# Feed forward: 24 of 32 inner tiles as twelve pairs of seven products each, kept in memory and loaded by output chunk

## The chip, the cores and the metric

One core of one Trainium2 chip. The metric is the device time of one execution, in microseconds (us). TensorE is called PE below, VectorE DVE, ScalarE ACT, GpSimd POOL and SyncE SP; SP issues most of the DMAs.

## What is computed

Two transformer-like blocks on one sequence of 1024 tokens by 1024 channels, all in fp32. The part that is changed is the feed forward of the first block, in the reference:

```
h = rmsnorm(x, norm_mlp_pre[l])
f = jnp.square(jax.nn.relu(h @ w_ff_in[l])) @ w_ff_out[l]
x = x + rmsnorm(f, norm_mlp_post[l])
```

`w_ff_in` is 1024 by 4096 and `w_ff_out` 4096 by 1024. The second block, behind it, has a wide projection of its own (`h @ w_in`), of which the kernel already forms a part with seven products instead of eight.

## The kernel before, in words

**Numbers.** Each fp32 operand is split in a high part (a rounded copy, made by ACT) and a low part (what is left, one subtraction on DVE). A product is three matmuls: high by high, high by low, low by high. Every matmul has a 128x128 stationary operand and 512 moving columns.

**Inner tiles.** An inner tile `("fi", T)` holds 128 of the 4096 inner channels for all 1024 tokens. The stationary operand is a slice of `w_ff_in`, the moving one the tokens `XBH`, `XBL` (high and low, in two halves of 512 tokens). `tile` (L2031) issues 8 depth slices x 2 halves x 3 = 48 matmuls (L2005 to L2007). It is then evicted on a chain of four steps, each of which waits for the one before: ACT relu from PSUM to `HS` (L1112), DVE square (L1628), ACT high copy to `H` (L1114), DVE low part (L1631). `H` has five places of one tile.

**Output chunks.** Chunk c (of eight, `FCH`) multiplies the inner tiles 4c to 4c+3 with the matching rows of `w_ff_out`: for both halves n of the 1024 output channels and for eight token groups m, `out_part` (L2318) issues 4 x 3 = 12 matmuls into one of four PSUM banks (`BANKS4`), so 192 to a chunk. The first chunk's results are copied to `F` by ACT (L1119), the others added to `F` by DVE (`f_add`, L1614). The weights of a half n live in `W2H[n]`, `W2L[n]`; their high copy (`hi`, L842) waits until the last part of that half of the chunk before is `filled`, their low part (`lo`, L1346) follows on DVE.

**Order.** The order of each engine is written out by hand. All four engines run the same loop over c (SP L653, ACT L1094, DVE L1619, PE L2346): the tiles 4c+1 to 4c+4, then chunk c. The tile 4c+4 stands between tile 4c+3 and chunk c. In the last round the tiles 29 to 31 stand between chunk 6 and chunk 7. Chunk 7 is issued in another order: for m = 0, 1 and both n the slices 0 to 2, then the four slices 3, then m = 2 to 7. While it runs, DVE and ACT finish the block (norm, sum, norm, `f_scale`, `x2_norm`) and PE turns the tokens (`t2_turn`, L2059).

**Waits.** `filled(key)` waits until PE has finished a result, `freed(key)` until it has been evicted. The two weight slots `raw` are filled by SP (`panel`, L472), each when the low part of the panel before last is made.

**The seven products.** In the second block `seven(p)` (L2427) makes two tiles of 128 channels from seven products of 512 tokens by 512 depth, 12 matmuls each (L2441 to L2443), 84 in place of 96. This needs four sums of token quarters, made once (`token_sum`, `TR` raw, `TH` high, `TL` low, each 128x2048), and four sums of weight quarters for each pair (`seven_sums`, `S`, 128x512). ACT copies three of the products to `c1`, `c5`, `c2`, DVE adds those to later ones into `stage` (three buffers of one tile), ACT applies the function, and SP stores the tile (`gate_store`). The weights of seven products go through a ring of four places (`seven_hi`, `seven_lo`).

## Time and profile before

| | us |
|---|---|
| median of 3 runs | 2179.26 (2177.72 to 2179.93) |
| the profiled execution's own time | 2176.35 |
| its span in the trace | 2174.6 |
| PE busy | 2140.1 |
| DVE busy | 1047.2 |
| ACT busy | 696.0 |
| mean DMA rate | 99 GB/s |

The feed forward runs from about 635 us (first inner tile) to about 1326 us (last output part), the seven products of the second block from 1471 to 1852 us. PE's busy time is of pipelined matmuls: a matmul is recorded with 0.39 us, though the next one starts 0.23 us after it. How fast PE works is read from the starts. The granted clock is 0.998 of full speed over the span.

### The profile page before, as it was taken

To read this page: it belongs to the slowest core of one execution; us is meant where nothing else is said; L and a number is where in the kernel's file an instruction comes from. 1 tells how busy PE (TensorE), PEld (TensorE's weight loads), DVE (VectorE), ACT (ScalarE), POOL (GpSimd) and SP (SyncE) were. 2 spreads that over 40 slices of the span, in tenths; PEclk is the share of its full clock that TensorE was granted. 3 is DMA by queue.
4 is the path that set the end of the run, shared out by engine and by line. 5 is a ranking of instruction groups with operands and counts; after the bars stand their busy time and mean duration, and the time that the engine had idled before them with its cause. 6 is when DMAs were issued, how large, how long until landed. Compare 5 with 4: busy or idle time off the path is not lost.

```text
span 2174.6 us, 24357 instructions
## 1 busy us (share of the span) xinstructions
PE 2140.1 (98%) x9972; PEld 1771.0 (81%) x9972; DVE 1047.2 (48%) x1170; ACT 696.0 (32%) x988; POOL 266.0 (12%) x507
## 2 busy tenths in 40 slices
PE   7999999999999999999999999999999999999998
PEld 6888888877888888888888888888888888878877
DVE  4226666847442233233232357666444566535452
ACT  4246666153233212112021135214444332222121
POOL 1376295000100000000000012100000000000100
PEclk9999999999999999999999999999999999999999
DMA  6542333676312012011020143212333221424332
GB/s 160 110 107 95 113 99 119 162 246 232 119 49 78 20 58 78 20 59 58 20 77 20 58 174 114 67 39 106 108 116 112 82 78 45 164 80 163 116 117 106
DMA packets 161922, 214.50 MB, mean 99 GB/s; under 512 B 26099, under 2 KB 127124, under 8 KB 161556
## 3 DMA queue, kind: packets, MB, share of 16 engines
q1 hardware_dynamic: 152336, 190.28, 26.9%
q10 hardware_dynamic: 9476, 22.67, 3.2%
q8 instruction: 79, 1.29, 0.2%
q14 instruction: 31, 0.25, 0.0%
HBM read 164.03 MB, written 47.71 MB: 97 GB/s over the span
## 4 chain that ended last, share of the span: by engine, by line
PE 86%; DVE 5%; issue 4%; ACT 2%; DMA 1%; SPq 1%; POOL 1%; DVEq 0%; POOLq 0%; ACTq 0%
PE A L2005 11%; PE A L2006 11%; PE A L2007 11%; PE X L2267 6%; PE X L2269 6%; PE X L2268 6%; PE X L2441 3%; PE X L2443 3%; PE X L2442 3%; PE A L2443 3%; PE A L2442 3%; PE A L2441 3%; PE A L2267 2%; PE A L2269 2%; PE A L2268 2%
## 5 line engine op out<-in xcount | busy, mean ns | idle before, releaser
L1339 DVE TENSOR_TENSOR WL<-raw,WH 128x1024 fp32r<-128x1024 f32 (+1 forms) x134 | 144.4, 1078 | 294.5 <-ACT WH L836 294.4
L2005 PE MATMUL A<-XBH,WH 128*128 128x512 f32 x616 | 240.1, 390 | 0.5 <-DVE WL L1339 0.5
L2007 PE MATMUL A<-XBH,WL 128*128 128x512 f32 x616 | 239.7, 389 | 0.0
L2006 PE MATMUL A<-XBL,WH 128*128 128x512 f32 x616 | 239.7, 389 | 0.0
L836 ACT ACTIVATE WH<-raw 128x1024 fp32r<-128x1024 f32 (+1 forms) x134 | 122.3, 913 | 282.4 <-PE A L2007 159.3
L2267 PE MATMUL X<-W2H,H 128*128 128x512 f32 x512 | 199.5, 390 | 0.0
L2269 PE MATMUL X<-W2H,H 128*128 128x512 f32 x512 | 199.2, 389 | 0.0
L2268 PE MATMUL X<-W2L,H 128*128 128x512 f32 x512 | 199.2, 389 | 0.0
L1112 ACT ACTIVATE HS<-A 128x1024 f32<-128x1024 f32 x32 | 32.8, 1024 | 400.9 <-PE A L2007 395.0
L2005 PE MATMUL A<-XH,WH 128*128 128x512 f32 x384 | 151.7, 395 | 0.0
L1618 DVE TENSOR_TENSOR F<-F,X 128x512 f32<-128x512 f32 x112 | 75.6, 685 | 156.3 <-PE X L2269 154.3
L2007 PE MATMUL A<-XH,WL 128*128 128x512 f32 x384 | 149.6, 390 | 0.0
L2006 PE MATMUL A<-XL,WH 128*128 128x512 f32 x384 | 149.5, 389 | 0.0
L2005 PEld LDWEIGHTS A<-XBH,WH 128*128 128x128 f32 x616 | 115.6, 188 | 25.0 <-issue 1.1
L2007 PEld LDWEIGHTS A<-XBH,WL 128*128 128x128 f32 x616 | 115.6, 188 | 24.1
L2006 PEld LDWEIGHTS A<-XBL,WH 128*128 128x128 f32 x616 | 115.6, 188 | 23.8
L1628 DVE TENSOR_TENSOR HS<-HS 128x1024 f32<-128x1024 f32 x32 | 39.1, 1223 | 171.7 <-ACT HS L1112 171.7
L2269 PEld LDWEIGHTS X<-W2H,H 128*128 128x128 f32 x512 | 96.1, 188 | 20.0
L2268 PEld LDWEIGHTS X<-W2L,H 128*128 128x128 f32 x512 | 96.1, 188 | 19.9
L2267 PEld LDWEIGHTS X<-W2H,H 128*128 128x128 f32 x512 | 96.1, 188 | 19.8
L1353 DVE TENSOR_TENSOR WL<-S,WH 128x512 fp32r<-128x512 f32 x80 | 55.1, 689 | 71.9 <-ACT WH L860 71.1
L2694 POOL TENSOR_TENSOR M<-M,GB 128x1024 f32<-128x1024 f32 x4 | 9.6, 2394 | 632.4 <-DVE GB L1919 632.4
(532 smaller groups left out, 4621.9 us busy)
## 6 DMA issues: line engine op xcount, KB each, us to landing
raw<-in_w_in SPq DMA_DIRECT2D x49, 1024.0 KB, 5.2
raw<-in_w_ff_in SPq DMA_DIRECT2D x16, 1024.0 KB, 5.4
rawk<-in_w_ff_out SPq DMA_DIRECT2D x16, 1024.0 KB, 5.0
g_scr<-stage SPq DMA_DIRECT2D x24, 512.0 KB, 3.6
g_scr<-gst ACTq DMA_DIRECT2D x32, 256.0 KB, 2.8
x_scr<-xr ACTq DMA_DIRECT2D x16, 512.0 KB, 2.6
xr<-x_scr SPq DMA_DIRECT2D x16, 512.0 KB, 4.2
xtok<-in_x SPq DMA_DIRECT2D x8, 512.0 KB, 7.4
```

What stands on the lines that cost most here:

```text
L836: A(unit_home(WH[:, r % 2, 0:kb, :], key), unit_of(raw[:, SLOT[p], 0:kb, :], key, i), ACT.Copy).then_inc(w_hi, 1)
L1339: TT(unit_home(WL[:, r, 0:kb, :], key), unit_of(raw[:, SLOT[p], 0:kb, :], key, i), unit_home(WH[:, r, 0:kb, :], key).bitcast(f32), ALU.sub ...
L1618: TT(F[:, m, sl], F[:, m, sl], psum(("fo", c, n, m)), ALU.add).then_inc(evicted[BUF["fo", c, n, m]], 1)
L2005: mm(dst, WH[:, r, k, :], xh, start=(k == 0), stop=False)
L2006: mm(dst, WH[:, r, k, :], xl, start=False, stop=False)
L2007: return mm(dst, WL[:, r, k, :], xh, start=False, stop=(k == kb - 1))
L2267: mm(dst, xh, wh(k), start=(k == 0), stop=False)
L2268: mm(dst, xh, wl(k), start=False, stop=False)
L2269: last = mm(dst, xl, wh(k), start=False, stop=(k == kb - 1))
L2441: mm(psum(key), high[:, i, :], xh, start=opens and i == 0, stop=False, skip_group_check=not opens)
L2442: mm(psum(key), high[:, i, :], xl, start=False, stop=False, skip_group_check=not opens)
L2443: last = mm(psum(key), low[:, i, :], xh, start=False, stop=i == KW - 1, skip_group_check=not opens)
```

## The change

Inner tiles 4 to 27 are made by `seven(p)`, p = 0 to 11, two to a pair; the tiles 0 to 3 (first) and 28 to 31 (last) stay plain. All 32 inner tiles are made before the first output chunk. The tiles 0 to 27 are evicted to `stage`, with relu on ACT and the square on DVE in place, and stored by SP to `h_scr` in memory, 512 KB each. Chunk 0 now uses the tiles 28 to 31, which stay in the SBUF; chunk c = 1 to 7 uses the tiles 4(c-1) to 4(c-1)+3, which SP loads (`h_load`) to `HBS`, where the tokens were, or to `HS`. ACT and DVE make their high and low parts in the middle of the chunk before, behind the weights of its first half. The token sums are formed on DVE during the plain tiles 0 to 3, each quarter from its high and low part (`rejoined`). In the second block the numbering of pairs and stages is shifted, its order is not. What is left out below is the counterpart of `seven_act`, `seven_dve` and `seven_func` for the new kind "f", and this shift.

```diff
-for _c in range(FCH):
-    if _c == 0:
-        pair("fi", 4)
-    if _c + 1 < FCH:
-        PANELS.append(([("fi", 4 * _c + 4), ("fi", 4 * _c + 5)], 1))
-    PANELS.append(([("w2", 2 * _c)], 1))
-    PANELS.append(([("w2", 2 * _c + 1)], 1))
-    if _c + 1 < FCH:
-        PANELS.append(([("fi", 4 * _c + 6), ("fi", 4 * _c + 7)], 1))
...
+SEVEN = [("f", i, 0) for i in range(2, 14)]
+SEVEN += [("g", s, i) for s in range(3) for i in range(4)] + [("b", i, kind) for i in range(2) for kind in range(4)]
+LAST_HIDDEN = 28
+
+RUNS = ((range(0, 12), "fi", (("fi", LAST_HIDDEN), ("fi", LAST_HIDDEN + 1))), (range(12, 32), "az", (("cx", 0), ("cx", 1))))
...
+pair("fi", 4)
+seven_panels(RUNS[0])
+for _i in range(LAST_HIDDEN, 4 * FCH, 2):
+    PANELS.append(([("fi", _i), ("fi", _i + 1)], 1))
+single("w2", 2 * FCH)
...
+FILLS += seven_fills(RUNS[0], (("A0a", "A0b", "X1a"), ("X0a", "X0b", "X1b")))
+FILLS += [(("fi", t), "A%d" % (t % 2)) for t in range(LAST_HIDDEN, 4 * FCH)]
...
-    FILLS += [(("fi", t), "A%d" % (t % 2)) for t in range(4 * _c + 5, min(4 * _c + 9, 4 * FCH))]
...
+        h_scr = dram("h_scr", [FF, SEQ])
...
+        def hidden_of(raw_form, u):
+
+            c, i = u // 4, u % 4
+            if c in (0, 2, 4, 7):
+                return (HS if raw_form else H)[:, (3, 4, 1, 0)[i]]
+            return (HBS if raw_form else HB)[:, i + (4 if c == 6 else 0)]
...
             def w2_panel(c, n):
-                panel(("w2", 2 * c + n), wf2[:, KW * c:KW * (c + 1), W4 * n:W4 * (n + 1)])
+                g = (c - 1) % FCH
+                panel(("w2", 2 * c + n), wf2[:, KW * g:KW * (g + 1), W4 * n:W4 * (n + 1)])
...
+            def h_store(T):
+                sp.wait_ge(hs_ready, T + 1)
+                sp.dma_start(h_scr[T * P:(T + 1) * P, :], stage[T % 3][:]).then_inc(x1_out[T % 3], 16)
+
+            def h_load(c):
+                if c in (2, 3, 4, 5, 7):
+                    filled(sp, ("fo", c - 3 if c == 7 else c - 2, 1, MT - 1))
+                for u in range(4 * c, 4 * c + 4):
+                    T = u - 4
+                    staged(sp, T % 3, T // 3 + 1)
+                    sp.dma_start(hidden_of(True, u)[:, 1, :], h_scr[T * P:(T + 1) * P, :]).then_inc(h_in[c % 2], 16)
+            for p in RUNS[0][0]:
+                seven_panel(p, wf1, 2 * P * (p + 2))
+                h_store(2 * p)
+                h_store(2 * p + 1)
+            fi_panel(LAST_HIDDEN)
+            h_store(LAST_HIDDEN - 4)
+            h_store(LAST_HIDDEN - 3)
+            fi_panel(LAST_HIDDEN + 2)
+            w2_panel(0, 0)
+            h_store(LAST_HIDDEN - 2)
+            h_store(LAST_HIDDEN - 1)
+            w2_panel(0, 1)
+            filled(sp, ("fi", 4 * FCH - 1))
+            for c in range(1, FCH):
+                h_load(c)
                 w2_panel(c, 0)
                 w2_panel(c, 1)
-                if c + 1 < FCH:
-                    fi_panel(4 * c + 6)
...
+            def hidden_stage(T):
+                filled(act, ("fi", T))
+                if T == 0:
+                    freed(act, ("t1", 7))
+                    for i in range(3):
+                        act.wait_ge(x1_out[i], STORED1[i])
+                staged(act, T % 3, T // 3)
+                A(stage[T % 3][:], psum(("fi", T)), ACT.Relu).then_inc(evicted[BUF["fi", T]], 1)
+            hi(("fi", 2))
+            hidden_stage(0)
+            sum_high(0, 0)
+            hi(("fi", 3))
+            hidden_stage(1)
+            sum_high(0, 1)
+            sum_high(0, 2)
+            seven_hi(0, 0)
+            seven_hi(0, 1)
+            hidden_stage(2)
+            sum_high(0, 3)
+            seven_hi(0, 2)
+            seven_hi(0, 3)
+            hidden_stage(3)
+            seven_run(0, None)
+
+            def hidden_high(u):
+                home = hidden_of(True, u)[:, 1, :]
+                if u < 4:
+                    act.wait_ge(hs_ready, LAST_HIDDEN + u + 1)
+                else:
+                    hidden_in(act, u // 4)
+                A(hidden_of(False, u)[:, 0, :], home, ACT.Copy).then_inc(hidden_hi, 1)
+            for i in range(3):
+                staged(act, i, (10, 9, 9)[i])
+            for u in range(4):
+                key = ("fi", LAST_HIDDEN + u)
+                if u in (1, 2):
+                    hi(("fi", LAST_HIDDEN + u + 1))
+                if u >= 2:
+                    hi(("w2", u - 2))
+                filled(act, key)
+                A(hidden_of(True, u)[:, 1, :], psum(key), ACT.Relu).then_inc(evicted[BUF[key]], 1)
+                hidden_high(u)
+            for c in range(FCH - 1):
+                for n in range(2):
+                    if c == 0:
                         for m in range(MT):
-                            filled(act, ("fo", 0, n, m))
-                            A(F[:, m, W4 * n:W4 * (n + 1)], psum(("fo", 0, n, m)), ACT.Copy
-                              ).then_inc(evicted[BUF["fo", 0, n, m]], 1)
+                            key = ("fo", 0, n, m)
+                            filled(act, key)
+                            A(F[:, m, W4 * n:W4 * (n + 1)], psum(key), ACT.Copy).then_inc(evicted[BUF[key]], 1)
+                    filled(act, ("fo", c, n, MT - 1))
+                    hi(("w2", 2 * (c + 1) + n))
+                    if n == 0:
+                        for u in range(4 * c + 4, 4 * c + 8):
+                            hidden_high(u)
             hi(("au", 0))
...
+            def hidden_square(T):
+                if T < 4:
+                    freed(dve, ("fi", T))
+                else:
+                    p, h = (T - 4) // 2, T % 2
+                    dve.wait_ge(stage_done, 3 * p + 3)
+                    if h:
+                        freed(dve, ("P", p, 6))
+                S = stage[T % 3][:]
+                TT(S, S, S, ALU.mult).then_inc(hs_ready, 1)
...
-            for c in range(FCH):
-                for T in range(0 if c == 0 else 4 * c + 1, min(4 * c + 5, 4 * FCH)):
-                    if T:
-                        follow(("fi", T))
-                    if T == min(4 * c + 4, 4 * FCH - 1):
-                        for n in range(2):
-                            lo(("w2", 2 * c + n))
-                    freed(dve, ("fi", T))
-                    S = HS[:, T % 5, 1, :]
-                    TT(S, S, S, ALU.mult).then_inc(hs_ready, 1)
-                    dve.wait_ge(hidden_hi, T + 1)
-                    dve.wait_ge(hs_ready, T + 1)
-                    TT(H[:, T % 5, 1, :], S, H[:, T % 5, 0, :].bitcast(f32), ALU.subtract).then_inc(hidden_lo, 1)
-                if 0 < c < FCH - 1:
-                    for n in range(2):
...
+            def quarter(t, k, h):
+                return t[:, h, KW * k:KW * k + KW, :].bitcast(f32)
+
+            def rejoined(dst, k, h):
+                return mark(TT(dst[:], quarter(XBH, k, h), quarter(XBL, k, h), ALU.add))
+
+            def sum_low(n, count):
+                dve.wait_ge(t_high, count)
+                TT(TL[n][:], TR[n][:], TH[n][:].bitcast(f32), ALU.subtract).then_inc(t_low, 1)
+            for m in (6, 7):
+                freed(dve, ("t1", m))
+            rejoined(TD[0], 0, 1)
+            link(TT(TD[1][:], quarter(XBH, 0, 0), quarter(XBL, 0, 0), ALU.add))
+            mark(TT(TR[0][:], TD[0][:], TD[1][:], ALU.subtract))
+            lo(("fi", 2))
+            hidden_square(0)
+            link(TT(TD[2][:], quarter(XBH, 1, 1), quarter(XBL, 1, 1), ALU.add))
+            TT(TR[2][:], TD[2][:], TD[0][:], ALU.subtract).then_inc(t_raw, 1)
+            dve.wait_ge(t_raw, 1)
+            TT(TR[1][:], TR[2][:], TD[1][:], ALU.add).then_inc(t_raw, 1)
+            lo(("fi", 3))
+            sum_low(0, 1)
+            hidden_square(1)
+            rejoined(TD[3], 1, 0)
+            after(chain[0])
+            dve.wait_ge(t_raw, 2)
+            TT(TR[3][:], TD[3][:], TR[1][:], ALU.subtract).then_inc(t_raw, 1)
+            dve.wait_ge(t_raw, 3)
+            sum_low(1, 2)
+            seven_sums(0, (0, 1))
+            seven_lo(0, 0)
+            seven_lo(0, 1)
+            sum_low(2, 3)
+            hidden_square(2)
+            seven_sums(0, (2, 3))
+            sum_low(3, 4)
+            seven_lo(0, 2)
+            seven_lo(0, 3)
+            hidden_square(3)
+            seven_run(0)
...
+            for u in range(4):
+                key = ("fi", LAST_HIDDEN + u)
+                if u in (1, 2):
+                    lo(("fi", LAST_HIDDEN + u + 1))
+                if u >= 2:
+                    lo(("w2", u - 2))
+                if u == 0:
+                    for T in (LAST_HIDDEN - 2, LAST_HIDDEN - 1):
+                        hidden_square(T)
+                freed(dve, key)
+                S = hidden_of(True, u)[:, 1, :]
+                TT(S, S, S, ALU.mult).then_inc(hs_ready, 1)
+                hidden_low(u)
+            for c in range(FCH - 1):
+                for n in range(2):
+                    if c:
                         for m in range(MT):
                             f_add(c, n, m)
+                    lo(("w2", 2 * (c + 1) + n))
+                    if n == 0:
+                        for u in range(4 * c + 4, 4 * c + 8):
+                            hidden_low(u)
             lo(("au", 0))
             lo(("au", 1))
 
...
                     pe.wait_ge(w_lo, UNIT["w2", 2 * c + n] + 1)
 
                 def tokens(k, m):
-                    s = (4 * c + k) % 5
-                    return H[:, s, 0, P * m:P * (m + 1)], H[:, s, 1, P * m:P * (m + 1)]
+                    home = hidden_of(False, 4 * c + k)
+                    return home[:, 0, P * m:P * (m + 1)], home[:, 1, P * m:P * (m + 1)]
 
                 def hidden(k):
...
-            for c in range(FCH):
-                for T in range(2 if c == 0 else 4 * c + 1, min(4 * c + 5, 4 * FCH)):
-                    tile(("fi", T), xb)
-                if c < FCH - 1:
-                    for n in range(2):
-                        for m in range(MT):
-                            out_part(c, n, m)
+            tile(("fi", 2), xb)
+            tile(("fi", 3), xb)
+            for p in RUNS[0][0]:
+                seven(p)
+            for T in range(LAST_HIDDEN, 4 * FCH):
+                if T == LAST_HIDDEN:
+                    for b in ("A0a", "A0b"):
+                        free_of(b, ("fi", T))
+                tile(("fi", T), xb)
+            for c in range(FCH - 1):
+                for n in range(2):
+                    for m in range(MT):
+                        out_part(c, n, m)
```

**DVE where the inner tiles begin.** `TD`, `TR`, `TL` are the token sums, `S` the weight sums, `WL` low parts of weights, `stage` an inner tile. Before, behind the last `XBL`:

```order
L1386 TENSOR_TENSOR XBL<-X,XBH 128x8x128 [waits xt_hi] x2
L1628 TENSOR_TENSOR HS<-HS 128x1024 [waits evicted_A0]
L1631 TENSOR_TENSOR H<-HS,H 128x1024 [waits hidden_squared,hidden_hi]
L1339 TENSOR_TENSOR WL<-raw,WH 128x1024 [waits w_hi]
L1628 TENSOR_TENSOR HS<-HS 128x1024 [waits evicted_A1]
L1631 TENSOR_TENSOR H<-HS,H 128x1024 [waits hidden_squared,hidden_hi]
L1339 TENSOR_TENSOR WL<-raw,WH 128x1024 [waits w_hi]
```

and with the change:

```order
L1816 TENSOR_TENSOR TD_198<-XBH,XBL 128x2048 [waits evicted_X1,evicted_X0]
L1824 TENSOR_TENSOR TD_199<-XBH,XBL 128x2048
L1825 TENSOR_TENSOR TR_190<-TD_198,TD_199 128x2048 [waits dve_chain]
L1427 TENSOR_TENSOR WL<-raw,WH 128x1024 [waits w_hi]
L1769 TENSOR_TENSOR stage_209<-stage_209 128x1024 [waits evicted_A0]
L1828 TENSOR_TENSOR TD_200<-XBH,XBL 128x2048
L1829 TENSOR_TENSOR TR_192<-TD_200,TD_198 128x2048 [waits dve_chain]
L1831 TENSOR_TENSOR TR_191<-TR_192,TD_199 128x2048 [waits t_sum]
L1427 TENSOR_TENSOR WL<-raw,WH 128x1024 [waits w_hi]
L1820 TENSOR_TENSOR TL_194<-TR_190,TH_186 128x2048 [waits t_hi]
L1769 TENSOR_TENSOR stage_210<-stage_210 128x1024 [waits evicted_A1]
L1816 TENSOR_TENSOR TD_201<-XBH,XBL 128x2048
```

Between the last token turn and the low weights of tile 2 there are now three operations of 2048 columns, and before the low weights of the third product (`WL<-S_203,WH`) there are twelve of them.

**DVE from the last plain tile to the first output chunks, with the change.** `HS` to `H` is the chain of an inner tile that stays in the SBUF, `HBS` to `HB` that of loaded tiles.

```order
L1434 TENSOR_TENSOR W2L<-rawk,W2H 128x2048 [waits w_hi]
L1870 TENSOR_TENSOR HS<-HS 128x1024 [waits evicted_A1]
L1857 TENSOR_TENSOR H<-HS,H 128x1024 [waits hidden_squared,hidden_hi]
L1434 TENSOR_TENSOR W2L<-rawk,W2H 128x2048 [waits w_hi]
L1857 TENSOR_TENSOR HB<-HBS,HB 128x1024 [waits hidden_hi] x4
L1434 TENSOR_TENSOR W2L<-rawk,W2H 128x2048 [waits w_hi]
L1810 TENSOR_TENSOR F<-F,X 128x512 [waits evicted_X0a,tile_done]
L1810 TENSOR_TENSOR F<-F,X 128x512 [waits evicted_X0b,tile_done]
```

The chain of tile 31 is the last thing ahead of chunk 0; before, one more tile stood between. The four loaded tiles stand between the weights of one half and the sums `F<-F,X` of the next.

**DVE at the last output chunk.** Before:

```order
L1346 TENSOR_TENSOR W2L<-rawk,W2H 128x2048 [waits w_hi] x2
L1628 TENSOR_TENSOR HS<-HS 128x1024 [waits evicted_A1]
L1631 TENSOR_TENSOR H<-HS,H 128x1024 [waits hidden_squared,hidden_hi]
L1339 TENSOR_TENSOR WL<-raw,WH 128x1024 [waits w_hi] x2
L1618 TENSOR_TENSOR F<-F,X 128x512 [waits evicted_X0a,tile_done,rows2_loaded]
```

and with the change:

```order
L1810 TENSOR_TENSOR F<-F,X 128x512 [waits evicted_X1b,tile_done]
L1434 TENSOR_TENSOR W2L<-rawk,W2H 128x2048 [waits w_hi]
L1427 TENSOR_TENSOR WL<-raw,WH 128x1024 [waits w_hi] x2
L1810 TENSOR_TENSOR F<-F,X 128x512 [waits evicted_X0a,tile_done,rows2_loaded]
L1810 TENSOR_TENSOR F<-F,X 128x512 [waits evicted_X0a,tile_done]
```

The low weights of half 1 of chunk 7 (`W2L`) and the two of `("au", 0)`, `("au", 1)` (`WL`) stood among the last inner tiles, and now stand directly behind the last sum of chunk 6. On ACT the high copies stand likewise. On SP the loads of `post2`, `pre3` and the `au` panel wait for the end of chunk 6, as before; three inner tiles came between that and chunk 7, and now none does.

## Rows read from the trace of the kernel before

**Rows 1.** The page's part 1: engine, busy us (share of span), instructions.
```profile
PE 2140.1 (98%) x9972; PEld 1771.0 (81%) x9972; DVE 1047.2 (48%) x1170; ACT 696.0 (32%) x988; POOL 266.0 (12%) x507
```

**Rows 2.** Windows: stretch, length, busy us of each engine, PEclk, DMA share, GB/s.
```profile
640.00:1278.00 638.00, 637.48 (x2813) 527.55 (x2812) 210.41 (x204) 131.44 (x125) 0.00 (x0) 1.00 0.15 51
1471.00:1852.00 381.00, 381.00 (x1682) 315.24 (x1680) 211.97 (x310) 149.38 (x257) 0.00 (x0) 1.00 0.27 95
```

**Rows 3.** PE's waits, 640 to 1345: us in total, times, longest.
```profile
PE A L2059 <- DVE F L1647: 0.5, 1, 0.5
PE A L2005 <- DVE WL L1339: 0.5, 1, 0.5
```

**Rows 4.** Timeline of PE in an inner tile: start, length, instruction; 36 matmuls apart.
```profile
665.79 0.39 PE L2005 MATMUL A<-XBH,WH 128*128 128x512 f32 x1
...
673.95 0.39 PE L2005 MATMUL A<-XBH,WH 128*128 128x512 f32 x1
```

**Rows 5.** Timeline of DVE where the inner tiles begin; in brackets the idle time before.
```profile
634.91 1.22 DVE L1386 TENSOR_TENSOR XBL<-X,XBH 128x1024 fp32r<-128x1024 f32 x1 [3.51 <-ACT XBH L879]
...
645.28 1.22 DVE L1339 TENSOR_TENSOR WL<-raw,WH 128x1024 fp32r<-128x1024 f32 x1
```

**Rows 6.** Timeline of ACT there and at the first output chunk.
```profile
646.17 1.02 ACT L1112 ACTIVATE HS<-A 128x1024 f32<-128x1024 f32 x1 [1.11 <-PE A L2007]
...
668.71 1.03 ACT L1112 ACTIVATE HS<-A 128x1024 f32<-128x1024 f32 x1 [6.55 <-PE A L2007]
671.03 1.06 ACT L1114 ACTIVATE H<-HS 128x1024 fp32r<-128x1024 f32 x1 [1.29 <-DVE HS L1628]
...
679.62 1.92 ACT L842 ACTIVATE W2H<-rawk 128x2048 fp32r<-128x2048 f32 x1 [4.77 <-PE A L2007]
```

**Rows 7.** Timeline of DVE where the second block prepares its products.
```profile
1355.81 2.28 DVE L1689 TENSOR_TENSOR TD<-XBH 128x2048 f32<-128x2048 f32 x1
1358.01 2.28 DVE L1692 TENSOR_TENSOR TR<-XBL 128x2048 f32<-128x2048 f32 x1
...
1451.60 0.69 DVE L1367 TENSOR_TENSOR S<-raw 128x512 f32<-128x512 f32 x1
```

**Rows 8.** The page's part 6, one issue: count, KB each, median us to landing.
```profile
g_scr<-stage SPq DMA_DIRECT2D x24, 512.0 KB, 3.6
```

**Rows 9.** Timeline of DVE at the first output chunk.
```profile
669.77 1.23 DVE L1628 TENSOR_TENSOR HS<-HS 128x1024 f32<-128x1024 f32 x1 [6.17 <-ACT HS L1112]
672.12 1.22 DVE L1631 TENSOR_TENSOR H<-HS,H 128x1024 fp32r<-128x1024 f32 x1 [1.13 <-ACT H L1114]
...
681.57 2.29 DVE L1346 TENSOR_TENSOR W2L<-rawk,W2H 128x2048 fp32r<-128x2048 f32 x1 [4.40 <-ACT W2H L842]
```

**Rows 10.** Timeline of SP's queue ahead of the last output chunk.
```profile
1262.03 0.37 SPq L472 DMA_DIRECT2D rawk<-in_w_ff_out  x1
...
1262.99 0.43 SPq L662 DMA_DIRECT2D pre<-in_norm_g  x1
1274.65 0.38 SPq L472 DMA_DIRECT2D raw<-in_w_in  x1
```

**Rows 11.** DMA issues, 1262 to 1300: count, KB each, median us to landing.
```profile
pre<-in_norm_g SPq DMA_DIRECT2D x1, 512.0 KB, 6.6
```

**Rows 12.** Timeline of DVE in the last output chunk.
```profile
1286.88 1.99 DVE L1618 TENSOR_TENSOR F<-F,X 128x512 f32<-128x512 f32 x3 [1.99 <-issue]
```

**Rows 13.** Windows: GB/s (last) over one chunk's stretch, and with DMAs queued.
```profile
657.00:700.00 43.00, 43.00 (x191) 35.61 (x190) 14.11 (x10) 15.73 (x17) 0.00 (x0) 1.00 0.22 74
1264.00:1266.00 2.00, 2.00 (x10) 1.65 (x9) 0.00 (x0) 0.00 (x0) 0.00 (x0) 1.00 1.04 401
```

**Rows 14.** Window of PE after its idle time at the start: busy, PEclk, DMA.
```profile
21.00:24.00 3.00, 2.48 (x6) 0.55 1.14 184
```

**Rows 15.** Timeline of PE there: 8 matmuls, then 8 more of the same size.
```profile
21.52 3.56 PE L2013 MATMUL X<-XH,WH 128*128 128x512 f32 x8 [3.49 <-ACT XH L879]
24.92 2.01 PE L2016 MATMUL X<-XH,WL 128*128 128x512 f32 x8
```

More of the change, by code:

```diff
@@ new lines, in sum_high, with seven_act @@
+            def sum_high(run, n):
+                act.wait_ge(t_raw, (1, 2, 2, 3)[n] if run == 0 else 3 + (1, 2, 4, 4)[n])
+                A(TH[n][:], TR[n][:], ACT.Copy).then_inc(t_high, 1)
+            def seven_act(p, j):
+                kind, i, n = SEVEN[p]
+                key = ("P", p, j)
+                if j in (0, 1, 2):
+                    filled(act, key)
+                    if p != run_of(p)[0][0]:
+                        freed(act, ("P", p - 1, 3 + j))
+                    A((c1, c5, c2)[j][:], psum(key), ACT.Copy).then_inc(evicted[BUF[key]], 1)
+                if j == 6 and (kind != "b" or n in (0, 3)):
+                    filled(act, key)
+                    if kind != "b":
+                        t = stage_of(p, 1)
+                        staged(act, t % 3, t // 3)
+                        dst, func = stage[t % 3][:], ACT.Sigmoid if kind == "g" else ACT.Relu
+                    elif n == 0:
+                        act.wait_ge(b_product if i else vec_out, 2 if i else 64)
+                        dst, func = Y[:, 2 * i + 1, :], ACT.Copy
+                    else:
+                        dst, func = Y[:, 2 * (1 - i) + 1, :], ACT.Silu
+                    A(dst[:, 0:HALF], psum(key), func).then_inc(evicted[BUF[key]], 1)
@@ new lines, in seven_func @@
+            def seven_func(p, j):
+                kind, i, n = SEVEN[p]
+                if kind == "b" and n != 3:
+                    return
+                h = int(j == 4)
+                dst = stage[stage_of(p, h) % 3][:] if kind != "b" else Y[:, 2 * (1 - i) + h, :]
+                dst = dst[:, 0:HALF] if j == 3 else dst[:, HALF:SEQ]
+                freed(act, ("P", p, j))
+                A(dst, dst, {"f": ACT.Relu, "g": ACT.Sigmoid, "b": ACT.Silu}[kind]
+                  ).then_inc(b_silu if kind == "b" else stage_done, 1)
@@ new lines, in seven_run @@
+            def seven_run(r, last_sum):
+                run, name, follow_keys = RUNS[r]
+                for p in run:
+                    for j in range(7):
+                        seven_act(p, j)
+                        if last_sum and p == run[0] and j == 0:
+                            last_sum()
+                            sum_high(r, 3)
+                        q = 7 * p + j + 4
+                        if q < 7 * run.stop:
+                            seven_hi(q // 7, q % 7)
+                        elif j in (4, 6):
+                            hi(follow_keys[j // 2 - 2])
+                        if j >= 4:
+                            seven_func(p, j - 1)
@@ L1230, in _ @@
[L1230 to L1242 removed]
+                    seven_hi(12, 2 * t - 4)
@@ L2316, in _, with high_low, summed, seven @@
             end(first_half(("fi", 1), xb, "t1", 1), ("fi", 1))
+            def high_low(k, h):
+                return lambda i: (XBH[:, h, KW * k + i, :], XBL[:, h, KW * k + i, :])
+            def summed(n):
+                return lambda i: (TH[n][:, i, :], TL[n][:, i, :])
+            MOVING = (high_low(0, 0), summed(0), summed(1), high_low(1, 0), summed(2), high_low(1, 1), summed(3))
+            def seven(p):
+                run = run_of(p)[0]
+                for j in range(7):
+                    key = ("P", p, j)
+                    if p - run[0] < 2 and j < 2:
+                        b = BUF[key][:2]
+                        free_of(b, key)
+                    begin(key)
+                    if p == run[0] and j in (1, 2, 4, 6):
+                        pe.wait_ge(t_low, {1: 1, 2: 2, 4: 3, 6: 4}[j] + (4 if p else 0))
+                    pe.wait_ge(w_lo, UNIT[key] + 1)
+                    high, low = seven_home(WH, p, j), seven_home(WL, p, j)
+                    opens = j in (0, 1, 3)
+                    for i in range(KW):
+                        xh, xl = MOVING[j](i)
+                        mm(psum(key), high[:, i, :], xh, start=opens and i == 0, stop=False, skip_group_check=not opens)
+                        mm(psum(key), high[:, i, :], xl, start=False, stop=False, skip_group_check=not opens)
+                        last = mm(psum(key), low[:, i, :], xh, start=False, stop=i == KW - 1, skip_group_check=not opens)
+                    end(last, key)
             def out_part(c, n, m, ks=range(KW)):
```

385 lines of the change are left out of this document (152 added, 233 removed).

## The prediction

> **What bounds the kernel now.** I read the page's shares first: PE is busy 98% of the span, DVE 48% and ACT 32% [rows 1]. The windows say the same of both stretches that matter: in the feed forward PE is busy 637.48 of 638 us, in the seven products of the second block 381 of 381, at the full granted clock [rows 2]. Of PE's waits over the whole feed forward only one of 0.5 us lies among the inner tiles, on the low weights of tile 2; another of 0.5 us lies at the first token turn of the last chunk [rows 3]. So time here is the number of matmuls, plus whatever makes PE wait. The price of a matmul is not the recorded 0.39 us but the distance of starts: 36 matmuls lie between two starts 8.16 us apart, 0.2267 us each [rows 4]. A product of the second block costs the same (381 us for 1680 matmuls, 0.2268) [rows 2]: seven products in a row run without a gap.
>
> **The matmuls.** Twelve pairs take 84 matmuls in place of 96: 144 fewer, 144 x 0.2267 = **-32.6 us**. The output chunks keep their 1536. Everything else is what PE has to wait for.
>
> **The start (tiles 0 to 3).** PE: the relu of tile 1 starts at 646.17 [rows 6]; it starts 0.43 behind the start of a tile's last matmul (a matmul's 0.39 and 0.04), so tile 2 could start at 645.97 and waits only because its low weights run from 645.28 to 646.50 [rows 5]. With the change ACT makes the high copy before the relu of tile 0, and on DVE only three sums stand ahead: from 634.91 + 1.14, three times 2.20 gives 642.7, low weights done at 643.9. The wait goes: **-0.5**. Tile 3 then starts at 656.85, the first product at 667.73, the third at 673.17 (two products of 12 matmuls).
> DVE up to the low weights of the third product: 12 operations of 2048 columns, 5 of 1024 (two weights, three squares), 7 of 512. In the second block two of 2048 start 2.20 apart though they last 2.28; one of 512 lasts 0.69 [rows 7]. Taking 0.08 off each: 12 x 2.20 + 5 x 1.14 + 7 x 0.61 = 36.4. Seven of them read what the one ahead wrote and start about 0.1 later: 0.7. One wait on ACT: its first high sum needs the second difference (about 649.7), lasts about 1.9, as W2H does [rows 6], and the high copy of tile 3's weights stands behind it (about 652.6, where DVE is at 651.9): 0.75. From 636.05 that makes 673.9, and PE takes the product at about 674.0, not 673.17: **+0.9**. Bounds: 0, and +3, if every one of the 24 operations pays 0.1. The first product is free: its low part stands at about 666.5, and bank A0 is evicted at 666.3.
>
> **The pairs.** Each adds two squares (2 x 1.22) to DVE, whose load in the run of the second block is 212 of 381 us, or 10.6 of a pair's 19.05 [rows 2]; 13.0 fits. The squares stand behind the low weights of products 4 and 5, needed two products later. A stage buffer must have been stored before it is written again: the square of a pair's first tile is done some 6 us into the next pair, a store takes 3.6 [rows 8], the buffer is written at about 13. I cost this at nothing. If a squared tile came 3 us later DVE would stop, and with it all weights.
>
> **Tile 31 and chunk 0.** Tile 4c+4 used to cover the chain of tile 4c+3. Now chunk 0 needs tile 31 at once. The chain, as it stands for tile 3: relu 668.71, square 669.77, high copy 671.03, low part 672.12 to 673.34 [rows 6, 9], so 4.63, plus 0.43 ahead of it and 0.06 behind. PE has three slices, 9 matmuls = 2.04 us, and the distance of one more: 5.12 - 2.27 = 2.85, with 0.1 for starting again **+3.0**. Bounds 2.5 and 3.5. Behind the last pair nothing is added: the stores of tiles 26 and 27 hold ACT for about 10 us, inside tile 28's 10.9.
>
> **The middle of chunks 1 to 6.** When half 0 is filled, DVE waits for ACT's W2H, makes W2L (4.24 us from the start of W2H: 679.62, 681.57 + 2.29 [rows 6, 9]), then four low parts (4 x 1.14), then adds the first part of half 1: done about 9.9 after the last matmul's start. PE wants that bank for the fifth part, 0.23 + 4 x 2.72 = 11.1. That leaves 1.2 us: nothing, if the data are there. The loads (2.1 MB of tiles, then 1 MB of weights) have 21.8 us, 144 GB/s; with DMAs queued the trace shows 401 GB/s [rows 13].
>
> **Chunk 7.** Before, its weights were made during tiles 29 to 31. Now half 1 can only be made when chunk 6 has ended, and PE asks for it after 9 matmuls: 0.43 + 4.24 + 0.06 - 2.27 = 2.46, with 0.1 **+2.6**; bounds 2.2 and 3. On DVE the low weights of `au` follow, whose panel is requested only now, behind post2 and pre3: together 2 MB, the amount that went in 7.6 us from 1262.03 on (the last request at 1262.99 lands 6.6 later) [rows 10, 11]; before, the panel was requested at 1274.65, three microseconds ahead of chunk 7. Panel at 8.1, two high copies and low parts to 11.9. The first sum of chunk 7 was taken at 1286.88 [rows 12], 39 matmuls after the chunk's start at 1277.8; with the stop it is due at 12.0. So it just fits. As DVE sets the first token turn already (0.5 us [rows 3]), what it loses is lost: I take **+0.3**, bounds 0 and +2.
>
> **A rule on the clock.** Near the start of the trace PE idles 3.49 us; the next 8 matmuls take 3.56 us and the 8 behind them 2.01 [rows 15], at a granted clock of 0.55 over 21 to 24 us [rows 14]: part of that stretch was at 1.2 GHz, the lower level, and cost 1.5 us. The Trainium skill (TensorE: Matmul & The Clock Gate, Part 1: The HAM clock gate) says that the array falls to half clock when it has been idle and comes back once it works. By it the two new waits could each be followed by a slow stretch, and the result would be some 3 us later. In the sum I take 0, since PE was busy at full clock for hundreds of microseconds before each and the waits are shorter than 3.49 us.
>
> **Sum.** -32.6 - 0.5 + 0.9 + 3.0 + 2.6 + 0.3 = **-26.3 us**. The profiled execution took 2176.35, so 2150.0 by its measure; the median of three is 2.9 above it, 2179.26, and against that the forecast is **2153.0 us**.
>
> **Rivals.**
> - *Late chunks.* The slack of 1.2 us in the middle of a chunk isn't there, because weights or loaded tiles land late, or each step waits a little more. For it: four more operations and four more DMAs per chunk in an order written by hand; against it: 401 GB/s. At 1.5 us in each of six chunks: +9, 2162.
> - *The clock falls* after the two waits: 2 x 1.5 = +3.1, 2156.
> - *The pairs stop.* Squares and stores come late and DVE holds the weights back by 1 us in each of twelve pairs: +12, 2165. Against it stand the 6 us of slack.
> - *Memory bounds the chunks, slower than before.* A chunk now moves 4.2 MB (four tiles, two panels) in 43.5 us. Decisive is 4.2 MB / 43.5 us = 96 GB/s: if stored tiles came back below that, every chunk would wait for them. At the 74 GB/s that the stretch 657 to 700 shows [rows 13] a chunk would take 56.7, seven of them 7 x 13.2 = +92: 2245. But 74 was what was asked for, not what could be had.
> - *Nothing gained*: that the products aren't issued. The order of instructions has 144 fewer matmuls, so I give it nothing of its own.
>
> **How the numbers follow.** Forecast 0.73, late chunks 0.11, clock 0.08, pairs stop 0.04, memory 0.02, something I don't see 0.02. Low end: both stops at their lower bounds, the start at 0, nothing at the tail: -33.1 + 4.7 = -28.4, 2150.9, and 3 us for the scatter between executions (2177.72 to 2179.93) and the uncertainty of stops I priced from above: 2148. High end: forecast with upper bounds (start +2.1, stops +0.9, tail +1.7) 2157.7, with the clock 2161, the late chunks 2162: 2163. A measurement of this kernel can tell about 0.2%, 4.4 us, from no change. Every case but the memory one lies over 14 us below: faster 0.96, same 0.02, slower 0.02.
>
> **What would show it.** In the profile after: 9828 matmuls; windows of twelve pairs of 19.05 us each with PE full; a wait of PE of about 3 us on DVE's low part of tile 31 ahead of chunk 0; one of about 2.5 us on W2L in chunk 7; one under 1 us ahead of the third product; no wait in the middle of chunks 1 to 6. I am wrong if PE waits for banks (sums of DVE) or DMAs there, if the first token turn comes more than 3 us later behind the start of chunk 7 than now, or if the granted clock dips behind a wait.

## The result, and the profile after

The change takes 2156.09 us (median of 4 runs, 2152.95 to 2157.00), the kernel before 2178.49 (4 runs): ratio 0.9892, interval 0.9879 to 0.9906, so 22.4 us or 1.1% faster. The forecast was 2153.0, the range 2148 to 2163. The profiled execution of the change took 2156.99, its span 2155.3.

The page's part 1 of the change (engine, busy us, share of the span, instructions), beside [rows 1]:

```profile
PE 2110.9 (98%) x9828; PEld 1746.7 (81%) x9828; DVE 1151.8 (53%) x1326; ACT 749.1 (35%) x1112; POOL 266.0 (12%) x507
```

144 matmuls fewer than [rows 1], and the share of PE is as high as before (PEld is the loading of stationary operands). Windows of the change, the first from inside the first pair to 6 us behind the last (stretch, length, busy us of PE, PEld, DVE, ACT and POOL, PEclk, DMA share, GB/s):

```profile
680.00:908.00 228.00, 228.00 (x1008) 188.87 (x1007) 134.45 (x187) 92.56 (x162) 0.00 (x0) 1.00 0.32 111
...
951.00:953.00 2.00, 2.00 (x7) 1.52 (x6) 0.00 (x0) 0.60 (x1) 0.00 (x0) 0.50 0.94 359
1260.00:1265.00 5.00, 5.00 (x23) 4.12 (x22) 0.00 (x0) 1.00 (x2) 0.00 (x0) 1.00 1.05 386
```

PE is busy throughout the first. The twelve pairs themselves run from 672.01 to 901.81: 229.80 us for 1008 matmuls, of which 1.04 is the wait of the third product listed next; the rest is 0.227 for each. PE's waits of the change over the whole feed forward (640 to 1325; us in total, times, longest), beside [rows 3]:

```profile
PE X L2422 <- DVE H L1857: 2.7, 1, 2.7
PE X L2422 <- DVE W2L L1434: 2.4, 1, 2.4
PE A L2214 <- DVE F L1892: 1.2, 1, 1.2
PE A L2214 <- DVE XBL L1474: 1.2, 1, 1.2
PE A L2496 <- DVE WL L1441: 1.0, 1, 1.0
PE X L2168 <- ACT XBH L935: 0.6, 1, 0.6
```

The third, fourth and sixth stood there before (0.5, 1.2 and 0.6; the last two, at the end of the feed forward, are not among the lines of [rows 3]). New are the three that were priced: tile 31's low part ahead of chunk 0, the weights in chunk 7, the third product. There is none in the middle of a chunk, though the page's part 6 shows slower loads: weights of an output chunk landed after 5.0 us before and after 9.3 now (medians); a store of a tile took 2.6.

```profile
rawk<-in_w_ff_out SPq DMA_DIRECT2D x16, 1024.0 KB, 9.3
h_scr<-stage SPq DMA_DIRECT2D x28, 512.0 KB, 2.6
```

**Where the time went.** The two profiles don't agree ahead of the feed forward, where the kernels are the same. I therefore measure the feed forward alone, as its *stretch*: from DVE's last low part of its tokens to the first low part of the second block's weights. Of the change, DVE's timeline at both ends:

```profile
639.20 1.23 DVE L1474 TENSOR_TENSOR XBL<-X,XBH 128x1024 fp32r<-128x1024 f32 x1 [3.51 <-ACT XBH L935]
...
1329.42 1.23 DVE L1427 TENSOR_TENSOR WL<-raw,WH 128x1024 fp32r<-128x1024 f32 x1 [6.96 <-ACT WH L891]
```

of the kernel before (its start is in [rows 5], 634.91):

```profile
1349.22 1.23 DVE L1339 TENSOR_TENSOR WL<-raw,WH 128x1024 fp32r<-128x1024 f32 x1 [6.98 <-ACT WH L836]
```

690.22 against 714.31: **24.1 us gained** where the sum said 26.3, and 4.3 us lost ahead of it.

Chunk 0's border is the part that came out otherwise. PE's timeline of the change:

```profile
945.33 0.39 PE L2422 MATMUL X<-W2H,H 128*128 128x512 f32 x1
...
950.22 0.79 PE L2422 MATMUL X<-W2H,H 128*128 128x512 f32 x1 [2.69 <-DVE H L1857]
...
951.24 0.63 PE L2424 MATMUL X<-W2H,H 128*128 128x512 f32 x1
951.66 0.63 PE L2422 MATMUL X<-W2H,H 128*128 128x512 f32 x1
...
953.86 0.39 PE L2422 MATMUL X<-W2H,H 128*128 128x512 f32 x1
```

The rows at 951.24 and 951.66 are neighbours, 0.42 apart where 0.227 is usual. From 945.33 to 953.86 lie 18 matmuls, 4.08 us at the usual distance; they took 8.53. So the border costs 4.45: the wait of 2.69, 1.56 for seven matmuls at the lower level (1.2 GHz; the window 951 to 953 has a granted clock of 0.50), 0.2 for starting again. Behind the wait of 2.39 in chunk 7 there is no such stretch: 1260 to 1265 stands at 1.00. In chunk 7, the queues of ACT, DVE and SP in the change:

```profile
1254.64 1.92 ACT L897 ACTIVATE W2H<-rawk 128x2048 fp32r<-128x2048 f32 x1 [16.05 <-PE X L2424]
1264.00 2.01 ACT L891 ACTIVATE WH<-raw 128x1024 fp32r<-128x1024 f32 x2 [7.43 <-DMA raw<-in_w_in]
```

```profile
1256.60 2.29 DVE L1434 TENSOR_TENSOR W2L<-rawk,W2H 128x2048 fp32r<-128x2048 f32 x1 [1.26 <-ACT W2H L897]
1265.09 2.36 DVE L1427 TENSOR_TENSOR WL<-raw,WH 128x1024 fp32r<-128x1024 f32 x2 [6.20 <-ACT WH L891]
```

```profile
1255.50 0.43 SPq L506 DMA_DIRECT2D raw<-in_w_in  x1
```

The panel of `au`, asked for at 1255.50, is there at 1264.00, where ACT's wait for it ends, 9.5 after the chunk's start at 1254.45 (forecast 8.1); DVE's first sum starts at 1267.37, where it was due about 12 after the start, 1266.5. From the chunk's start to the first token turn it took 25.99 us (1254.45 to 1280.44), before 22.45 (1277.79 to 1300.24): +3.5.

### The profile page after: what moved, and what is told of

Its sections match the earlier page's. It is cut to its first block, busy times and chain, and to the rows that moved or that the text cites. A ratio compares the mean times of both kernels' runs of the same rounds, so it can differ in the third digit from the quotient of the medians.

```text
span 2155.3 us, 24566 instructions
## 1 busy us (share of the span) xinstructions
PE 2110.9 (98%) x9828; PEld 1746.7 (81%) x9828; DVE 1151.8 (53%) x1326; ACT 749.1 (35%) x1112; POOL 266.0 (12%) x507
## 4 chain that ended last, share of the span: by engine, by line
PE 83%; DVE 7%; issue 4%; ACT 2%; DMA 1%; SPq 1%; POOL 1%; DVEq 0%; POOLq 0%; ACTq 0%
PE A L2160 7%; PE A L2162 7%; PE A L2161 7%; PE X L2422 6%; PE X L2423 6%; PE X L2424 6%; PE X L2497 5%; PE X L2496 5%; PE X L2498 5%; PE A L2497 4%; PE A L2496 4%; PE A L2498 4%; PE X L2160 2%; PE A L2422 2%; PE A L2423 2%
## 5 line engine op out<-in xcount | busy, mean ns | idle before, releaser
L2496 PE MATMUL X<-TH,WH 128*128 128x512 f32 x280 | 109.1, 390 | 0.0
L2498 PE MATMUL X<-TH,WL 128*128 128x512 f32 x280 | 109.1, 389 | 0.0
L2497 PE MATMUL X<-TL,WH 128*128 128x512 f32 x280 | 109.0, 389 | 0.0
L2422 PE MATMUL X<-W2H,H 128*128 128x512 f32 x256 | 101.1, 395 | 5.1 <-DVE H L1857 2.7
L2423 PE MATMUL X<-W2L,H 128*128 128x512 f32 x256 | 100.3, 392 | 0.0
L2424 PE MATMUL X<-W2H,H 128*128 128x512 f32 x256 | 100.3, 392 | 0.0
L2423 PE MATMUL X<-W2L,HB 128*128 128x512 f32 x256 | 99.7, 390 | 0.0
L2424 PE MATMUL X<-W2H,HB 128*128 128x512 f32 x256 | 99.7, 390 | 0.0
L2422 PE MATMUL X<-W2H,HB 128*128 128x512 f32 x256 | 99.7, 389 | 0.0
L2496 PE MATMUL A<-TH,WH 128*128 128x512 f32 x232 | 90.4, 390 | 1.0 <-DVE WL L1441 1.0
L2160 PE MATMUL A<-XBH,WH 128*128 128x512 f32 x232 | 90.8, 391 | 0.0
L2162 PE MATMUL A<-XBH,WL 128*128 128x512 f32 x232 | 90.4, 390 | 0.0
```

The lines of the kernel that those rows point to most:

```text
L2160: mm(dst, WH[:, r, k, :], xh, start=(k == 0), stop=False)
L2162: return mm(dst, WL[:, r, k, :], xh, start=False, stop=(k == kb - 1))
L2422: mm(dst, xh, wh(k), start=(k == 0), stop=False)
L2423: mm(dst, xh, wl(k), start=False, stop=False)
L2424: last = mm(dst, xl, wh(k), start=False, stop=(k == kb - 1))
L2496: mm(psum(key), high[:, i, :], xh, start=opens and i == 0, stop=False, skip_group_check=not opens)
```

## The experiments

Each time is compared with runs of the kernel before on the same chip (2178.75 for experiments 1 to 4, 2179.82 for 5 to 7 and 9, and a single run of 2178.63 for 8). The stretch is that of each profile.

**1. The first chunk in split order** (`s1`).

```
+            for ks in (range(KW - 1), (KW - 1,)):
+                for m in range(4):
+                    out_part(0, 0, m, ks)
...
-                    for m in range(MT):
+                    for m in range(4 if c == 0 and n == 0 else 0, MT):
```

> The feed forward is measured from the last low part of its tokens (VectorE, 639.20 us in the profile of the change, 634.91 before) to the first low part of the second block's token-mixing weights (1329.42; 1349.22 before): 690.2 us in the change, 714.3 before. Here the first output chunk runs the inner slices 0 to 2 for four token parts (36 matmuls, 8.2 us) before it takes slice 3, whose low part comes 4.8 us after the chunk's start. Theory: the 2.7 us wait on that low part and the half-clock matmuls behind it (7 of 0.43 us where 0.227 is usual, 1.5 us) are one cost of the order and both go: stretch 686.0, time 4.2 us under the change's. Rival 1: the half clock has nothing to do with the wait and stays: stretch 687.5. Rival 2: another operand is as late (a bank, slice 2): stretch 690.2.

Measured: 2151.83 (2150.08 to 2153.36), ratio 0.9872 (0.9857 to 0.9888), stretch 685.6. The window over the border of that kernel (PE busy 13.00 of 13.00, granted clock 1.00):

```profile
947.00:960.00 13.00, 13.00 (x59) 10.78 (x58) 2.45 (x2) 4.48 (x6) 0.00 (x0) 1.00 0.86 323
```

4.6 us under the change, by expectation 4.2: wait and half clock went together, and with them the 0.2 of the restart. Where the wait is gone there is no half clock in this profile; the first rival and the second fall.

**2. The last chunk's order of parts alone** (`s2`; the list of banks follows the order and is left out).

```
-            for ks in (range(KW - 1), (KW - 1,)):
-                for m in range(2):
-                    for n in range(2):
-                        out_part(FCH - 1, n, m, ks)
+            for n in range(2):
+                for m in range(2):
+                    out_part(FCH - 1, n, m)
```

> The last output chunk takes both token parts of the first half of its columns whole (24 matmuls, 5.4 us) before it needs the second half's weights, whose low part comes 4.6 us after the chunk's start. Naive theory: the 2.4 us wait on those weights goes, stretch 687.8. My theory: behind it stands the first sum of the chunk, which VectorE can't begin before the tail weights' panel has landed and been split (its end 13.6 us after the chunk's start in the change); its bank is wanted again 48 matmuls = 10.9 us after the start, so a wait of some 2.7 us on F takes the place of the one removed: stretch 690.0 to 690.5.

Measured: 2155.41 (2155.08 to 2155.80), ratio 0.9892 (0.9878 to 0.9905), stretch 691.2. PE's timeline of that kernel:

```profile
1266.64 0.80 PE L2423 MATMUL X<-W2H,H 128*128 128x512 f32 x1 [2.85 <-DVE F L1811]
```

and its window just behind:

```profile
1267.00:1272.00 5.00, 5.00 (x13) 3.85 (x13) 3.33 (x5) 1.79 (x6) 0.98 (x3) 0.50 1.08 355
```

The wait on the weights is gone and one on the bank stands in its place, 39 matmuls further on: 2.85 us, near the 2.7 expected. It is followed by 13 matmuls at half clock, 2.9 us more than their usual time, which I hadn't expected. DVE's last operation ahead of the first token turn, and the turn itself:

```profile
1277.64 1.28 DVE L1893 SCALAR_TENSOR_TENSOR F<-xr,vec,pre 128x1024 f32<-128x1024 f32 x1
```

```profile
1280.46 1.03 PE L2215 MATMUL A<-ident,F 128*128 128x128 f32 x8
```

PE comes to the turn 1.54 us after DVE is done and no longer waits there, nor on XBH behind it, so only 1.0 of the slow stretch reaches the end (691.2 against 690.2). Without it PE would have been 2.9 earlier and would have waited for DVE: the turn would stand about 26.2 us behind the chunk's start at 1252.76, where it stood 25.99 in the change (an estimate from these rows). Two late things stood in series; removing the first alone gives nothing.

**3. That order, and the panel asked for earlier** (`s3`: experiment 2 and this).

```
-            filled(sp, ("fo", FCH - 2, 1, MT - 1))
             sp.dma_start(post2[:], ...
...
             panel(("au", 0), w2[:, :, A_U:A_U + 256])
+            filled(sp, ("fo", FCH - 2, 1, MT - 1))
```

> As the last, and the two norm rows and the tail's first panel are asked for as soon as the panel's slot is free (inside the chunk before the last, some 7 us sooner) instead of at the last chunk's start. My theory: the panel lands before the last chunk's weights are split, first sum some 8 us after the chunk's start, so both the 2.4 us wait on the weights and 0.7 us of the first token turn's 1.2 us go: stretch 687.1, time 3 us under the change's. Rival: the sums are bound by VectorE's own queue, and the first token turn waits as long as now: stretch 687.8 to 690.

Measured: 2150.62 (2147.38 to 2151.73), ratio 0.9867 (0.9854 to 0.9881), stretch 685.3, 5.0 under the change. ACT's timeline of that kernel, then DVE's:

```profile
1254.42 1.92 ACT L898 ACTIVATE W2H<-rawk 128x2048 fp32r<-128x2048 f32 x1 [16.05 <-PE X L2425]
1256.24 1.99 ACT L892 ACTIVATE WH<-raw 128x1024 fp32r<-128x1024 f32 x2
```

```profile
1260.85 0.68 DVE L1811 TENSOR_TENSOR F<-F,X 128x512 f32<-128x512 f32 x1
```

ACT finds the panel in place and goes on without idle time; the first sum starts 6.6 us after the chunk's start (1254.22), not 12.9. PE has no wait at all between 1240 and 1300. The panel was asked for at 1236.93, 17.3 us ahead of the chunk (1254.22), where I had expected some 7. I had let half a microsecond of the token turn stand and not thought of the bank wanted before it (0.3) nor of the 0.6 on XBH behind it: all went, with the restarts, hence 5.0 and not 3.1.

**4. Plain tiles, stored and loaded** (`s4`): the twelve pairs undone, with their sums of tokens and weights, and the stores, the loads and the order of chunks kept.

```
-            for p in RUNS[0][0]:
-                seven(p)
-            for T in range(LAST_HIDDEN, 4 * FCH):
...
+            for T in range(2, 4 * FCH):
                 tile(("fi", T), xb)
```

> All 28 stored inner tiles are plain ones (48 matmuls each), with the change's storing, loading and order of chunks: the products alone are undone, 144 matmuls more. Theory A (the products give what their matmuls are worth, and storing costs only the waits seen at the two borders): 32.6 us more than the change, less the 1.0 us wait before the third product: stretch 721.8, some 7.5 over before; time 31.6 us over the change's. Theory B (the products have a price of their own beside the matmuls, in sums or banks): a difference to the change of under 31, stretch under 721. Theory C (storing and loading delay matmuls in plain tiles, where stores come at the same rate): stretch over 723.

Measured: 2188.01 (2187.26 to 2188.73), ratio 1.0041 (1.0028 to 1.0054), stretch 721.5. PE's waits of that kernel over its feed forward:

```profile
PE X L2374 <- DVE H L1809: 2.7, 1, 2.7
PE X L2374 <- DVE W2L L1419: 2.4, 1, 2.4
PE A L2166 <- DVE F L1844: 1.2, 1, 1.2
```

Theory A: 721.8 was expected. The products alone give 31.3 us (721.5 - 690.2), 144 matmuls less the wait of the third product; storing and the new order alone cost 7.2 over before (714.3). That is the change in two parts: -31.3 and +7.2 make -24.1. The 7.2 are the two borders, less tile 2's wait of 0.5, which is gone here too: the same waits of 2.7 and 2.4 us are here, without any product, and half clock stands behind the first.

**5. Everything covered** (`s5`: experiments 1 and 3, and the third product's weights made earlier on ACT and DVE, as in experiment 7).

> All covers together: the first output chunk in split order over four token parts, the last chunk's order of parts, the rows and the tail's first panel asked for early, and the third product's low weights made before a hidden tile's square and two sums. Theory (the costs of the order are separate places and add): the stretch of the feed forward is the change's 690.2 less 4.6 (as the split order gave), 5.0 (as the last chunk's cover gave) and 1.0: 679.6 us, so time some 10.6 under the change's. Rival (one wait covers another, or VectorE's queue turns up elsewhere): over 681.

Measured: 2146.14 (2143.82 to 2147.48), ratio 0.9844 (0.9831 to 0.9858), stretch 679.4. The window over the feed forward of that kernel:

```profile
642.00:1306.00 664.00, 664.00 (x2954) 550.03 (x2953) 362.79 (x408) 212.35 (x305) 23.24 (x40) 1.00 0.31 111
```

PE is busy 664.00 of 664.00 us at full clock. The three costs add as expected, and this version is 10 us faster than the change.

**6. The waits made longer and shorter** (`s6`).

```
+            out_part(0, 0, 0, range(KW - 1))
+            out_part(0, 0, 1, range(1))
+            out_part(0, 0, 0, (KW - 1,))
+            out_part(0, 0, 1, range(1, KW))
...
-            for ks in (range(KW - 1), (KW - 1,)):
+            for ks in (range(2), range(2, KW)):
```

> So far matmuls at half clock stood behind each wait of 2.7 us in the first chunk (4 of 4 profiles) and the one of 2.85 us in the last, and behind none of the 2.4 us waits in the last chunk (4 of 4). Here the first chunk runs 12 matmuls before it needs slice 3 (9 in the change), so its wait is 2.0 us, and the last chunk runs 6 before it needs the second half's weights (9 in the change), so its wait is 3.1 us. If the length of the wait decides: no half clock in the first chunk, and matmuls of 0.43 us behind the wait in the last. If the place decides (what stands before or behind it): half clock in the first chunk still, none in the last. The stretch is 689.9 by the first and 690.2 by the second, so the rows tell, not the time.

Measured: one run, 2158.00, stretch 690.6. PE's timeline of that kernel:

```profile
951.63 0.76 PE L2422 MATMUL X<-W2H,H 128*128 128x512 f32 x1 [2.10 <-DVE H L1857]
...
1259.81 0.76 PE L2422 MATMUL X<-W2H,H 128*128 128x512 f32 x1 [3.06 <-DVE W2L L1434]
```

and its windows behind the two:

```profile
952.00:954.00 2.00, 2.00 (x6) 1.52 (x6) 0.00 (x0) 0.60 (x1) 0.00 (x0) 0.50 0.99 392
1260.00:1265.00 5.00, 5.00 (x12) 3.90 (x13) 0.00 (x0) 0.00 (x0) 0.00 (x0) 0.50 1.04 357
```

Half clock behind both. Neither theory survives, the length of the wait or its place alone: 2.10 us in the first chunk was enough where 2.39 in the last was not, and in the last chunk 3.06 was.

**7. The third product's weights alone** (`s7`). On DVE (on ACT the high copy goes ahead of one sum):

```
             sum_low(2, 3)
+            seven_lo(0, 2)
             hidden_square(2)
             seven_sums(0, (2, 3))
             sum_low(3, 4)
-            seven_lo(0, 2)
             seven_lo(0, 3)
```

> Only the third product's low weights are made earlier on VectorE, and their high part on ScalarE. Theory: its wait of 1.0 us goes and nothing takes its place, stretch 689.2. Rival: the work pushed behind (a square, two sums) makes a later product of the first pair wait as long: 690.2.

Measured: one run, 2155.20, stretch 687.3: 2.9 us gained, not 1.0. The wait of the third product is gone and none has come in its place, but most of the other 1.9 is the half clock, which is missing here (it cost 1.56 in the change):

```profile
950.76 0.50 PE L2422 MATMUL X<-W2H,H 128*128 128x512 f32 x1 [2.69 <-DVE H L1857]
951.10 0.40 PE L2423 MATMUL X<-W2L,H 128*128 128x512 f32 x1
951.33 0.39 PE L2424 MATMUL X<-W2H,H 128*128 128x512 f32 x1
```

Here the same wait of 2.69 us ahead of slice 3 is followed by matmuls 0.23 apart, at full clock.

**8. The same kernels again** (`a1`, `a2` the change, `a3` experiment 7; no edit).

> The change, word for word, profiled a second time. Its 2.69 us wait ahead of slice 3 of the first chunk was followed by matmuls of 0.43 us in five profiles of five different kernels, after waits of 2.10 to 2.69 us, and in one kernel (only the third product's weights made earlier) a wait of the same 2.69 us was not. Theory 1: which execution shows it is a matter of chance, whatever the kernel: of this kernel's two further profiles and one more of the other, at least one differs from that kernel's first. Without the half clock the stretch is 688.7, with it 690.2. Theory 2: it belongs to the kernel: here half clock again, stretch 690.2.

> The change a third time, with the same expectations: 688.7 or 690.2 by the first theory, 690.2 by the second. The 2.4 us wait of the last chunk is followed by none (5 of 5 so far), if a shorter wait makes it rarer; by the first theory one may show it there.

> The kernel with the third product's weights earlier, a second time. Theory 1: half clock or not, stretch 689.0 or 687.3. Theory 2 (it belongs to the kernel): none, 687.3.

Measured: 2157.40, 2155.75 and 2153.20; stretches 690.6, 690.7 and 689.4. The change showed the half clock in all three profiles, the kernel of experiment 7 in its second (`a3`) and not in its first. The timeline of `a3`:

```profile
946.71 0.50 PE L2422 MATMUL X<-W2H,H 128*128 128x512 f32 x1 [2.69 <-DVE H L1857]
...
947.52 0.40 PE L2422 MATMUL X<-W2H,H 128*128 128x512 f32 x1
947.76 0.56 PE L2423 MATMUL X<-W2L,H 128*128 128x512 f32 x1
948.12 0.63 PE L2424 MATMUL X<-W2H,H 128*128 128x512 f32 x1
```

So it doesn't belong to the kernel, and the slow matmuls need not begin at the wait: here four ran at full clock first. With the half clock in both, moving the third product's weights gives 690.5 (mean of the change's three) less 689.4, 1.1 us, as first expected. Behind the 2.4 us wait in the last chunk PE ran at full clock in all seven profiles that have it.

**9. The kernel before, again** (`b1`).

> The kernel before, word for word, profiled again. The part ahead of the feed forward is the same in both kernels, yet its last low part began at 634.9 us in the profile of before and at 639.2 in that of the change (637.4 to 640.9 in four kernels with the same start). Theory: this is scatter of executions, and the profile of before was a quick one (2176.35 against a median of 2178.8): the mark comes at 636 to 640 here, and the stretch is 714.3. Rival: the hidden rows' memory, which only the change has, sets other addresses and delays the loads ahead of the feed forward: the mark comes at 634 to 636 again.

Measured: 2180.42 (11 runs, 2177.58 to 2182.26), ratio 1.0002 (0.9993 to 1.0011). Its DVE timeline:

```profile
641.15 1.23 DVE L1386 TENSOR_TENSOR XBL<-X,XBH 128x1024 fp32r<-128x1024 f32 x1 [3.51 <-ACT XBH L879]
...
1355.51 1.23 DVE L1339 TENSOR_TENSOR WL<-raw,WH 128x1024 fp32r<-128x1024 f32 x1 [6.96 <-ACT WH L836]
```

The mark comes at 641.15, 6.2 later than in the first profile of the same program and a little beyond the 636 to 640 expected; the stretch is 714.4, the same to 0.1. The 4.3 us ahead of the feed forward are scatter of executions: over the profiles of all kernels with this start the mark lies between 634.9 and 641.3. The hidden rows' memory isn't needed to explain it.

## Why the prediction was right, and where it was off

The time came out 3.1 us above the forecast, inside the range: 2.2 us of the stretch (24.1 gained, not 26.3), 1.7 outside it, less 0.8 because the kernel before had a median of 2178.49 here and of 2179.26 when the forecast was made. By its own steps, against the stretch:

- **The matmuls**, -32.6: right. The pairs run 1008 matmuls in 229.80 us less the wait of 1.04, 0.227 each, and undoing them costs 31.3 where 32.6 - 1.0 - 0.2 = 31.4 was due.
- **Tile 2's wait**, -0.5: gone, as forecast.
- **The third product**, +0.9: 1.04 of wait, 1.2 with the restart by the rows, 1.1 by experiment.
- **The pairs**, 0, and **the middle of the chunks**, 0: right. The load of an output chunk's weights took 9.3 us and not 5.0, and still nothing waited for it. The late chunks, the stopped pairs and the memory bound didn't happen.
- **Tile 31 and chunk 0**, +3.0: the wait itself was 2.69 with 0.2 behind it, but the term was 4.45. This is the step that failed: "In the sum I take 0, since PE was busy at full clock for hundreds of microseconds before each and the waits are shorter than 3.49 us." The reason doesn't hold: the half clock came although PE had been busy at a granted clock of 1.00 for hundreds of microseconds (the window 680 to 908 above, and on to 945), and in experiment 6 behind only 2.10 us. The rival that names it had the size of one stretch right (1.5, measured 1.56), but it comes once and not twice; its chance of 0.08 was too low, since the stretch stands in 8 of 9 profiles with a wait at this place. That its 2156 meets the measured 2156.09 is luck: 1.56 of its 3.1 us is there, and the rest comes from the tail and from outside the feed forward.
- **Chunk 7**, +2.6 and **the tail**, +0.3: together 2.9, measured 3.5. The wait on the weights was 2.39 (2.46 forecast). The tail was mis-sized: the panel landed 9.5 and not 8.1 us after the chunk's start, which makes 0.6 at the first token turn (1.17 against 0.53) and some 0.3 at the bank wanted before it.
- **Its own signs of being wrong**: two of them came, the granted clock that dips behind a wait and a first token turn more than 3 us later behind the start of chunk 7 than before (3.5).

Sum, with the matmuls at their price and the rest as measured: -32.6 - 0.5 + 1.2 + 4.45 + 3.5 = -24.0, and the stretch says 24.1. The medians differ by 1.7 us less (22.4). That lies outside the stretch, where both kernels do the same work and where the start of the stretch alone scatters by 6 us between executions; with 4 runs of each I can't say whether any of these 1.7 us is more than that.

## What to carry to other kernels

Price a removed wait by what is late next: in the last chunk the weights and the panel were late one behind the other, and curing the weights alone gave nothing. Where a stage loses the work that covered its hand-over, cut the next stage's first parts so that all of them run up to the slice that is late before any of them takes it; here 36 matmuls instead of 9 hid the whole chain. And ask for a panel when its slot is free, not when the stage before it ends: here the queue's order of waits kept the request back to 1 us behind the chunk's start, and with the request 18.3 us sooner (experiment 3) no wait was left.

## What the runs showed of the hardware

Waits of PE of 2.1 to 3.1 us can be followed by matmuls at the lower clock level, 1.2 GHz (granted clock 0.50, starts 0.43 us apart), though PE had run at 2.4 for hundreds of microseconds. Behind the wait in the first chunk (2.10 to 2.69 us) half clock stood in 8 of 9 profiles and cost 1.6 to 1.7 us each time; behind 2.39 us in the last chunk it stood in none of 7; behind 2.85 and 3.06 there it stood in both and cost 2.9 and 2.7 us. Behind the waits of 0.3 to 1.2 us in the same profiles it stood nowhere. Where a border had no wait (experiments 1, 3 and 5) there was none. The same kernel showed it once and once not, and once it began a microsecond after work had been taken up again. The Trainium skill (TensorE: Matmul & The Clock Gate, Part 1: The HAM clock gate) describes the watch on the array's activity as free-running, so not started by the program; the rows agree with that, but no run here shows what decides, and why the 2.4 us in the last chunk never had it stays open. Until it is known, I price a wait of PE of 2 to 3 us at its length plus 0 to 3 us.
